# A skewed bias table built from sixteen rows instead of 128 and read in eight pieces, with two attention heads one place later

## The reference, cut to what matters

```python
h = rms_norm(x, pre_mix_norm[l])
proj = h @ w_in[l]                      # 2048 x 5656
(dq, dk, dv, nq, kc, vc, ksl, vsl, kwn, vwn, g) = jnp.split(proj, offsets, axis=-1)
o_diff = diff_attention(q_d, k_d, v_d, lam, lam_init, subln[l], bias_diff)   # 8 heads
k_c = compress(kc, cmp_pos_k[l], cmp_k_w1[l], cmp_k_w2[l])
v_c = compress(vc, cmp_pos_v[l], cmp_v_w1[l], cmp_v_w2[l])
o_nsa = nsa_attention(q_n, k_c, v_c, k_s, v_s, k_w, v_w, gates, bias_nsa)    # 8 heads
x = x + rms_norm(concatenate([o_diff, o_nsa]) @ w_out[l], post_mix_norm[l])

def compress(k, pos_emb, w1, w2):       # blocks of 32 tokens, one every 16
    blocks = k[:, idx] + pos_emb[:, None, :]
    return jax.nn.gelu(blocks.reshape(B, G, nc, 32 * d) @ w1, approximate=True) @ w2
```

## Time and profile before

| | |
|---|---|
| median of 3 runs | 2399.59 us (2397.59 to 2401.9) |
| the profiled execution | 2398.08 us, its span 2396.3 us |
| PE busy | 2326.6 us, 97% of the span |
| DVE busy | 1462.1 us, 61% |
| ACT busy | 1142.6 us, 48% |
| POOL busy | 56.7 us, 2% |
| DMA packets, mean | 422.39 MB, 176 GB/s |
| granted TensorE clock, mean of the span | 0.992 |

### The profile page before, as it was taken

How to read it: one execution, slowest core, us unless ns; L and a number is a source line. 1 busy time by engine, 2 the same in 40 slices (tenths; PEclk the granted TensorE clock), 3 DMA queues, 4 the chain that set the end, 5 groups by cost and what they waited for, 6 DMA issues and landing times.

```text
span 2396.3 us, 33680 instructions
## 1 busy us (share of the span) xinstructions
PE 2326.6 (97%) x12330; PEld 1962.6 (82%) x12330; DVE 1462.1 (61%) x1893; ACT 1142.6 (48%) x1612; POOL 56.7 (2%) x81
## 2 busy tenths in 40 slices
PE   6799999999999999999999999999999999999997
PEld 5588878788888888888878888877888888888886
DVE  4355566567777446776566668866566444566544
ACT  4254455465555445555454564445444434444432
POOL 2200000000000000000010000000000000000000
PEclk9899999999999999999999999999999999999999
DMA  8974445556556566556556453354665656665652
GB/s 180 310 229 123 141 132 167 167 161 195 180 186 193 193 192 184 182 177 212 192 156 184 123 167 106 97 174 147 199 184 184 193 192 190 188 185 185 210 193 96
DMA packets 322022, 422.39 MB, mean 176 GB/s; under 512 B 13438, under 2 KB 232888, under 8 KB 321156
## 3 DMA queue, kind: packets, MB, share of 16 engines
q1 hardware_dynamic: 315968, 398.70, 53.7%
q0 software_dynamic: 5376, 20.19, 3.3%
q10 hardware_dynamic: 580, 2.20, 0.3%
HBM read 415.80 MB, written 5.25 MB: 176 GB/s over the span
## 4 chain that ended last, share of the span: by engine, by line
PE 83%; issue 7%; DMA 4%; DVE 4%; ACT 2%; POOL 0%; DVEq 0%; SPq 0%; POOLq 0%; ACTq 0%
PE PS L1784 23%; PE PS L1785 12%; PE PS L1750 7%; PE PS L1749 7%; PE PS L1748 7%; PE PS L1845 4%; PE PS L2101 3%; DMA stage<-in_w_in 2%; PE PS L1859 2%; PE PS L1861 2%; PE PS L1860 2%; PE PS L1846 2%; PE PS L2102 2%; PE PS L2112 1%; PE PS L2114 1%
## 5 line engine op out<-in xcount | busy, mean ns | idle before, releaser
L1784 PE MATMUL PS<-actT,whi 128*128 128x512 f32 x2432 | 859.8, 397 | 1.8 <-DVE wlo L1152 1.8
L1785 PE MATMUL PS<-actT,wlo 128*128 128x256 f32 x2432 | 683.4, 281 | 0.0
L1784 PEld LDWEIGHTS PS<-actT,whi 128*128 128x128 f32 x2432 | 457.2, 188 | 115.1 <-DVE wlo L1152 2.1
L1152 DVE TENSOR_TENSOR wlo<-stage,whi 128x1024 fp32r<-128x1024 f32 x298 | 362.7, 1223 | 237.0 <-ACT whi L730 236.9
L1123 DVE TENSOR_TENSOR wlo<-stage,whi 128x1024 fp32r<-128x1024 f32 x245 | 298.9, 1226 | 306.0 <-ACT whi L672 306.0
L730 ACT ACTIVATE whi<-stage 128x1024 fp32r<-128x1024 f32 x298 | 315.9, 1061 | 319.9 <-PE PS L1785 306.2
L1785 PEld LDWEIGHTS PS<-actT,wlo 128*128 128x128 f32 x2432 | 456.5, 188 | 0.1
L672 ACT ACTIVATE whi<-stage 128x1024 fp32r<-128x1024 f32 x245 | 258.3, 1059 | 349.7 <-PE PS L1750 324.9
L1750 PE MATMUL PS<-whi,gT 128*128 128x512 f32 x864 | 340.4, 394 | 0.0
L1749 PE MATMUL PS<-wlo,gT 128*128 128x512 f32 x864 | 338.7, 392 | 0.0
L1748 PE MATMUL PS<-whi,gT 128*128 128x512 f32 x864 | 335.2, 388 | 0.0
(11 more groups left out here) (332 smaller groups left out, 2787.3 us busy)
## 6 DMA issues: line engine op xcount, KB each, us to landing
stage<-in_w_up SPq DMA_DIRECT2D x304, 512.0 KB, 3.8
stage<-in_w_down SPq DMA_DIRECT2D x216, 512.0 KB, 4.4
stage<-in_w_in SPq DMA_DIRECT2D x160, 512.0 KB, 3.8
stage<-in_w_out SPq DMA_DIRECT2D x64, 512.0 KB, 3.7
DQK<-in_cmp_k_w POOLq DMA_DIRECT2D x8, 512.0 KB, 21.6
stage<-in_w_in SPq DMA_DIRECT2D x16, 256.0 KB, 3.9
DQK<-in_cmp_v_w POOLq DMA_DIRECT2D x8, 512.0 KB, 5.9
bias_by_distance<-work POOLq DMA_DIRECT2D x1, 3072.0 KB, 33.7
```

Source lines behind the costliest of these rows:

```text
L1152: nc.vector.tensor_tensor(wlo[:, j % SPLITS, :], stage[:, j, :], whi[:, j % SPLITS, :].bitcast(F32), ALU.subtract).then_inc(ev("lo_done"), 1)
L1784: nc.tensor.matmul(o, whi[:, j % SPLITS, at], actT[:, k, :], start=k == 0, stop=False)
L1785: last = nc.tensor.matmul(o[:, S:2 * S], wlo[:, j % SPLITS, at], actT[:, k, 0:S], start=False, stop=k == KC - 1)
```

## The change

Three edits. The table has 16 copies of each row instead of 128, and is written before the first reciprocal root, where GpSimd had nothing to issue. It is read in eight DMAs of 16 partitions each, one behind each of `compress_in(4)` to `compress_in(11)`; GpSimd's blocks thus come ahead of every read of the table. The last two heads of `DIFF_AT` stand one tile later, and what hangs on them with them.

```diff
-DIFF_AT = {71 + 3 * r: r for r in range(HD)}
+DIFF_AT = {71: 0, 74: 1, 77: 2, 80: 3, 83: 4, 86: 5, 90: 6, 93: 7}
...
+            pool.wait_ge(ev("urow"), 2)
+            pool.dma_start(scratch, urow.rearrange("h (o k) -> h o k", o=1).broadcast_to((16, 16, SK))).then_inc(ev("scratch_out"), 16)
             inv_sqrt(1, small[:, 4:6], small[:, 2:4], 2)
...
             pool.wait_ge(ev("actlo_n1"), KC)
-            pool.wait_ge(ev("urow"), 2)
-            pool.dma_start(scratch, urow.rearrange("h (o k) -> h o k", o=1).broadcast_to((16, P, SK))).then_inc(ev("scratch_out"), 16)
             for j in range(4):
                 compress_in(j)
-            pool.wait_ge(ev("scratch_out"), 16)
-            pool.dma_start(bias[:, :, :], bass.AP(scratch.tensor, P - 1, [[SK - 1, P], [P * SK, 16], [1, S]])).then_inc(ev("bias_in"), 16)
-
             pool.wait_ge(ev("cols"), 1)
...
+            pool.wait_ge(ev("scratch_out"), 16)
             for j in range(4, 16):
                 compress_in(j)
+                if j < 12:
+                    at = 16 * (j - 4)
+                    pool.dma_start(bias[at:at + 16, :, :], bass.AP(scratch.tensor, P - 1 - at, [[SK - 1, 16], [16 * SK, 16], [1, S]]))\
+                        .then_inc(ev("bias_in"), 16)
...
-                if n in (97, 98):
-                    diff_high(n - 97)
+                if n in (98, 99):
+                    diff_high(n - 98)
...
-                    dve.wait_ge(ev("bias_in"), 16)
+                    dve.wait_ge(ev("bias_in"), 16 * 8)
...
-                if n in (98, 99):
-                    diff_low(n - 98)
+                if n in (99, 100):
+                    diff_low(n - 99)
...
-                if n in (94, 105):
+                if n in (95, 105):
                     diff_chunks(n // 105)
...
-    scratch = nc.dram_tensor("bias_by_distance", (16, P, SK), F32, kind="Internal").ap()
+    scratch = nc.dram_tensor("bias_by_distance", (16, 16, SK), F32, kind="Internal").ap()
```

## The result

The changed kernel takes 2386.4 us against 2399.6 us (medians of five executions each). The forecast was 2386. One execution of the changed kernel took over three times as long (8140 us) and was disturbed; without it the median is 2385.4, and the ratio of the means is 0.9937, with a 95% interval of 0.9921 to 0.9952. The profiled execution took 2384.42 us, its span 2382.6 us, 13.7 us less than the span before.

What follows compares the result with a forecast made beforehand. TensorE was taken to be bound by waits on GpSimd's blocks, held up by the slow table write, and on VectorE's join. 2398.1 - 17.9 + 7 + 1 - 2.9 = 2385.3; median 1.5 above, forecast 2386, range 2375 to 2395.

Steps and rivals of the forecast that it cites:

- The first gap: TensorE between tile 8 and tile 16: 40.4 us against 22.5 undisturbed; 17.9 go, 14.7 of them idle.
- what would show it wrong: Signs: fast reads, third tile landing at 20 or later, long waits at the last heads, or uncounted compression-weight waits.
- The eight reads: Table reads on q0, 2.8 us each, make tile 26's weights late: +7 us, between 0 and 13.
- the ledger: Count of q0 and q1 transfers until 98.9 us: weights short by 0.3 MB, tile 26 late by about 4.8 us.
- Rival 1: Tiles 20 to 27: the table reads stay hidden and cost nothing, 2377 us; chance 0.27.
- Rival 4: Tiles 20 to 27: reads still slower, 5.5 us each at half of 95 GB/s, 2407 us; chance 0.04.
- The write at the start: Early table write delays the third weight tile and so the first product: +1 us, between 0 and 4.1.
- The heads: Last two heads one tile later fill TensorE's wait ahead of diff_scores(6): -2.9 us, between 0 and -6.0.
- rival 2: At the start, the table's write delays the first product by all of its 4 us, 2389 us; chance 0.12.

Runs made afterwards that it cites:

- The order alone: Kernel before, with GpSimd awaiting and reading the table behind its blocks and two small loads, table still 128 copies: 2396.9 us, ratio 0.9996.
- the kernel with the write late: Changed kernel with the table's write behind the first reciprocal root instead of ahead of it: 2381.3 us, ratio 0.9932.
- The moved copy: Changed kernel with ScalarE's copy of the first compression result out of PSUM ahead of tile 28's split: 2381.5 us, ratio 0.9930.

## Why the prediction was right, and where not

**The first gap, -17.9: measured -17.8.** The work in it was counted from undisturbed tiles, and that is what came back. The reason was only half told. The prediction followed the wait to GpSimd's blocks and named the tile weights behind the write as a second victim; it did not name the compression weights on the same queue, and said under what would show it wrong that it had not counted waits for them. The order alone showed them: with the blocks 22 us early the wait shrank from 14.7 to 12.4. So the cause of the gap is the write on q0, with two victims, and the place of the read in GpSimd's order, which the prediction put first, did not matter once the write was small and early.

**The eight reads, +7: measured +7.0,** 4.41 us idle and 2.6 at the lower clock (5.6 us of work at 0.50 from 110.8 to 116.4 would make 2.8), where 4.8 and 2.2 were forecast. That is one execution; in the kernel with the write late the same reads cost 4.1 us, and by the ratios they cost some 5.5 in the mean, so the match to a tenth is luck. The sum also hit closer than its parts deserve, since several of them were off. A read takes 2.2 us in an emptier stretch and 2.5 in its own place, not 2.8: the nearest row, the write at 95 GB/s, was 10 to 20% slower than the reads. Beside a read q1 gets 36 GB/s (0.50 MB in 14 us), not the 20 that stand in the earlier trace rows; but beside a load and a read together only 0.77 MB in 15 us, 51 GB/s, where the ledger gave it 80 beside a load and 350 in what was left. And q0 is not served first, as the ledger had it: from 95 to 110 us q0 and q1 move 746 and 745 packets. q1's are of 1.0 KB there, q0's of 3.5 KB, and so a slow read holds q1 back by packets and not by bytes. With 2.5 us a read and 36 GB/s beside it the ledger would have shown no stall at all (3.2 MB for q1 where 2.6 are needed); its faults cancelled. The second miss is the place. Tile 27's weights landed at 104.3 and were split by 106.6, just after TensorE was done at 106.38: a wait of 0.3 us. The other 4 us are tile 28's landing at 109.7, which reached TensorE one tile early, because ScalarE held the copy for `part_out` behind it. The moved copy shows that this only changes where the debt is paid.

Rival 1 (reads hidden, 2377) was what happens as soon as a read takes 1.4 us (reads eight apart, 2379.3) or is put where the queues are half empty (2379.0). The point from which it decides was given as 2.0 us, which does not follow from the ledger: short by 0.3 MB at 2.8 us, it comes out even at some 2.6. In the runs the point lies between 1.4 and 2.5. The Trainium skill, SBUF — State Buffer, section Door 1: The DMA port swizzle, says that sixteen neighbours reach four of the sixteen ports; by its table sixteen partitions eight apart reach eight, and 32 four apart all of them. The trace agrees in order and at the upper end and not in proportion: 119, 186 and 318 GB/s beside q1's equal packets, where four, eight and sixteen ports would make it 1 to 2 to 4.

Rival 4 (slower than before) was rightly far off, but its price was too high: the ledger made each further microsecond of a read about 8 us of stall, and 1.4 us more gave at most 9.3 instead of 11, some 6 in the mean. Even at 3.6 us a read the kernel stays ahead of the one before (0.9963).

**The write at the start, +1: not shown.** The profiled execution has +1.21, and on the chain that was named: ScalarE splits the third tile at 18.08 instead of 16.99. It looked like the term, but seven profiles with the early write and seven without differ by -0.3 us in the mean, give or take 0.9. No such term shows, in a start that varies by more.

**The heads, -2.9: measured -3.5 and, alone, -3.6.** The waits of 1.40 us and 1.03 us and the clock of 1.00 are what was forecast. VectorE's idle time had more to give back than the 1.9 us that were counted: from the join to the end of `diff_front(7)` it took 19.10 us instead of 19.76, with the split and the pair more, so 2.6 us of idle time were won back.

**The sum:** -17.9 + 7 + 1 - 2.9 = -12.8 against -13.7. With the 1.5 us from the profiled execution to the median it gives 2386.8, not the 2386 that was forecast. The start's +1.2, the 1.6 us of low clock in the kernel before, and the 1.0 us behind the region are luck of the two executions and not the change; they nearly cancel.

## What to carry to other kernels

When a wait goes, ask for each of the things that the waiting instruction needs when it was there: a queue that held up one of them often held up the others as well, and the profile names only the last. A DMA to few partitions is slow by which partitions it touches; spreading the same pieces over the partitions (every eighth, every fourth) cost nothing and removed the stall, and the slow form did no harm either in a stretch where the queues had room. Before two changes are both called needed, try each alone: here the one that the profile pointed at, the order, did nothing alone, and the gap went without it. Do not pay for a late weight by moving what waits for it: the debt comes due at a later tile, with its clock.

## What had not been expected of the hardware

- q0 and q1 move equal numbers of packets while both have work (507 and 506, 457 and 457, 746 and 745, and 802 and 808 in the earlier trace rows). A queue with small packets therefore loses bytes to one with large or slow ones. The Trainium skill, DMA: Bandwidth & Descriptors, section Queues, rings and completion order, has the engines take one whole packet from each queue in turn. The counts here agree, if its packets are the ones that the profile counts, which no run shows. The prediction has the rule in its rival 2 and left it out of its ledger.
- GpSimd's additions and VectorE's splits slow each other. Beside VectorE's work four additions take 4.76 us at 48.15 (1.19 each), where they took 0.79 in the earlier trace rows, and 0.68 (four in 2.73 at 58.87) in the kernel with the order alone, where VectorE had nothing to do; and VectorE's splits beside them take 1.63 us instead of the 1.23 of the earlier trace rows. VectorE's timeline of the changed kernel:

```profile
48.32 1.63 DVE L1470 TENSOR_TENSOR wlo<-stage,whi 128x1024 fp32r<-128x1024 f32 x1 [0.26 <-ACT whi L925]
50.66 1.65 DVE L1470 TENSOR_TENSOR wlo<-stage,whi 128x1024 fp32r<-128x1024 f32 x1 [0.71 <-ACT whi L925]
...
59.63 1.63 DVE L1470 TENSOR_TENSOR wlo<-stage,whi 128x1024 fp32r<-128x1024 f32 x1 [0.26 <-ACT whi L925]
```

In the kernel before, where eight additions ran without a pause, they lost little (0.79 against 0.68 each) and the split beside them a lot:

```profile
73.74 3.64 DVE L1468 TENSOR_TENSOR wlo<-stage,whi 128x1024 fp32r<-128x1024 f32 x1 [15.58 <-ACT whi L923]
```

Both engines had slack in the changed kernel, so it cost nothing there. The Trainium skill, SBUF — State Buffer, section SBUF: two separate sides, says that GpSimd and VectorE with two inputs in SBUF hold a shared pair of ports in turn, each for a whole instruction. The rows agree that they hold each other up; why the loss is shared in one kernel and falls nearly all on VectorE in the other stays open.

- TensorE's granted clock falls now and then between 180 and 220 us in unbroken work (0.91 in 200 to 220 us of the kernel before, 0.83 in 180 to 200 us with the copy moved, 1.00 in the changed kernel), in 8 of the 14 profiles. It costs 1.6 us at 0.91: the times to the turn are 418.3 to 418.4 without it and 419.9 with it. What sets it off stays open.
